# A list scheduler for the order of every engine, and byte addresses for the experts, in a two-layer encoder on eight cores

## The reference

```python
def reference(x, ...):
    h = x
    for layer in range(2):
        y = rmsnorm(h, norm_mix_g[layer])
        y = pool_attn_mixer(y, ...) if layer == 0 else sgu_mixer(y, ...)
        h = h + y
        h = h + hier_moe(rmsnorm(h, norm_ffn_g[layer]), ...)
    return rmsnorm(h, final_norm_g)

def pool_attn_mixer(h, w_in, w_pool, pool_scale, rel_bias, w_out):
    z = h @ w_in                      # 1024 x 2048: pooled channels, q, k, v
    ...                               # window means 2/4/8/16; 8 heads, own 64-frame chunk and 8 before it
    return concatenate([a_out, b_out], -1) @ w_out

def sgu_mixer(h, w_in, b_in, ln_g, ln_b, w_s, b_s, w_out):
    u, v = split(gelu(h @ w_in + b_in), 2, axis=-1)
    v = layernorm(v, ln_g, ln_b)      # then a lower-triangular 128 x 128 mix over positions, per head
    ...
    return (u * mixed) @ w_out

def hier_moe(h, ...):                 # router: best of 4 groups, best 2 of its 4 experts
    act = silu(h @ w_gate) * (h @ w_up) * combine     # 16 experts of width 256, two per token are not zero
    return act @ w_down
```

## Time and profile before

| | us |
|---|---|
| median of 3 runs | 3680.98 (3679.82 to 3682.50) |
| the profiled execution | 3689.05 |
| its span on the slowest core | 3687.1 |
| spans of the eight cores | 3668.3 to 3687.1 |

### The profile page before, as it was taken

One profiled execution on the slowest core, in us unless ns is written; L12 is line 12 of the kernel. 1 busy time (PEld: TensorE's weight loads), 2 busy tenths in 40 slices (PEclk: granted clock), 3 DMA queues, 4 the chain that ended last, 5 costly groups with the idle time before them and its releaser, 6 DMA issues. The chain is left out here.

```text
span 3687.1 us, 37878 instructions; the slowest of 8 cores (3668.3 to 3687.1 us)
## 1 busy us (share of the span) xinstructions
PE 2436.4 (66%) x10190; PEld 1001.2 (27%) x10374; DVE 1357.0 (37%) x2933; ACT 1158.2 (31%) x1864; POOL 565.7 (15%) x860
## 2 busy tenths in 40 slices
PE   0665755647574663888888466575666648888886
PEld 0222322223232231222222133343333322222221
DVE  1343433334343442222222153344443433333333
ACT  1353444444443531222222132322332212333332
POOL 1000000010000012222222111110111122333332
PEclk9876876778676776999999777777777769999998
DMA  9001101010110054355431311111111272453200
GB/s 197 23 30 39 46 23 49 20 65 27 46 37 21 29 100 91 80 116 121 106 88 45 87 35 63 63 52 69 43 50 57 59 151 77 112 129 108 68 23 1
DMA packets 88263, 243.91 MB, mean 66 GB/s; under 512 B 22360, under 2 KB 31064, under 8 KB 87568
## 3 DMA queue, kind: packets, MB, share of 16 engines
q0 software_dynamic: 57840, 130.65, 16.6%
q1 hardware_dynamic: 30240, 110.83, 9.0%
HBM read 516.19 MB, written 94.50 MB: 166 GB/s over the span
## 5 line engine op out<-in xcount | busy, mean ns | idle before, releaser
L303 PE MATMUL psum<-arena 128*128 128x512 bf16 x2979 | 836.3, 440 | 37.9 <-DVE arena L907 10.9
L610 PE MATMUL psum<-arena 128*128 x1722 | 668.9, 391 | 188.5 <-issue 106.9
L303 PEld LDWEIGHTS psum<-arena 128*128 128x128 bf16 x3072 | 327.4, 111 | 498.4 <-issue 227.1
L293 POOL TENSOR_SCALAR arena<-arena 128x1 f32<-128x1 f32 x215 | 88.3, 411 | 2075.2 <-ACT arena L391 1123.1
L373 PE MATMUL psum<-arena 128*128 128x128 bf16 x512 | 65.5, 308 | 457.0 <-DVE arena L366 381.7
L632 PE MATMUL psum<-arena 128*128 x844 | 318.5, 390 | 46.9 <-issue 4.5
L610 PEld LDWEIGHTS psum<-arena 128*128 128x128 bf16 x1760 | 168.4, 96 | 662.2 <-issue 662.2
L614 DVE SCALAR_TENSOR_TENSOR arena<-arena,psum 128x256 bf16<-128x256 f32 x220 | 105.7, 480 | 562.7 <-ACT arena L612 334.6
L612 ACT ACTIVATE arena<-psum 128x256 f32<-128x256 f32 x220 | 84.5, 384 | 625.8 <-PE psum L610 520.8
L898 PE MATMUL psum<-arena 128*128 128x512 bf16 (+3 forms) x469 | 132.7, 349 | 174.7 <-DVE arena L884 141.8
L635 DVE TENSOR_TENSOR arena<-psum,arena 128x1024 f32<-128x1024 f32 x110 | 134.7, 1225 | 291.9 <-PE psum L632 291.9
(11 more groups left out here) (170 smaller groups left out, 2785.7 us busy)
## 6 DMA issues: line engine op xcount, KB each, us to landing
arena<-wmoe POOLq DMA_DIRECT2D x114, 1536.0 KB, 46.4
arena<-x SPq DMA_DIRECT2D x64, 512.0 KB, 3.4
H<-arena SPq DMA_DIRECT2D x64, 512.0 KB, 2.8
arena<-H SPq DMA_DIRECT2D x64, 512.0 KB, 3.3
arena<-ab_w_in POOLq DMA_DIRECT2D x4, 1024.0 KB, 55.0
arena<-sgu_w_in POOLq DMA_DIRECT2D x4, 1024.0 KB, 11.7
TBL<-arena SPq DMA_DIRECT2D x2, 1536.0 KB, 23.4
arena<-gvec SPq DMA_DIRECT2D x5, 512.0 KB, 11.0
```

The costliest lines, as they stand in the source:

```text
L293: P.add("pool", lambda e: e.tensor_scalar(out=rs, in0=ss, scalar1=scale, scalar2=EPS, op0=ALU.mult, op1=ALU.add), reads=kss, writes=krs)
L303: P.add("pe", lambda e, kc=kc: e.matmul(bank(b), lhsT=lhs(kc), rhs=rhs(kc), start=(kc == 0), stop=(kc == n - 1)), reads=reads(kc), writes= ...
L610: return e.matmul(bank(b), lhsT=tT[i % 2][:, kc, :], rhs=W[:, bass.ds(v + kc * 512, 512)], start=(kc == 0), stop=(kc == 7))
```

## The change

`Prog` keeps one list of all operations. Before anything is emitted, `schedule` runs a list scheduler over the whole program: each operation has an estimated duration and latency (`estimate`, or a pair given with `add`), DMAs share one rate, and at each step the operation that can start earliest is taken, among at most 48 of an engine whose predecessors are placed; an earlier place in the program wins where starts are equal. PSUM banks are chosen there as well: a `VT` stands for a bank, or a pair, out of an allowed set, and gets it when its first operation is placed. `waits` then works out which semaphore waits are needed, leaving out those that an earlier wait implies. The hand-made interleaving is gone: the program lists stage 1, attention and output projection of a super-block in plain order, the same in layer 1, and the steps of an item one after the other in `moe`.

The expert slots are addressed in bytes, and the constant part of an address goes into the slice. The two Exp of `route` become powers of e on POOL. The last item also names all six slots as read.

```diff
+def estimate(eng, fn):
+    r = Rec(); fn(r)
+    n, a, k = r.call
...
+    if n.endswith("dma_start"):
...
+        return (1000 if eng == "pool" else 70), byts
...
+    if eng == "pe":
+        if n == "transpose":
+            f32 = a[1].dtype == F32
+            return (215 if f32 else 57), 170
+        f32 = k["lhsT"].dtype == F32
+        return (max(200, sz * 4 / 2.4) if f32 else max(57, sz / 2.4 + 3)), 170
+    if eng == "act":
+        return ((172 if ps else 224) + sz) / 1.2, 60
+    if eng == "dve":
+        return ((120 if ps else 62) + sz) / 0.96, 60
+    return 400 + sz * 1.1, 60
...
+        def pick(e):
+            best = None
+            T = free_t[e]
+            n = 0
+            for idx, op in avail[e]:
+                n += 1
+                if n > 48:
+                    break
+                st = max(T, ready[op])
+                new = [v for v in (op.vt or ()) if v.banks is None]
+                if new:
+                    if any(d.fin is None for v in new for d in v.ext):
+                        continue
+                    pl = place(new[0])
+                    if pl is None:
+                        continue
+                    st = max(st, pl[0])
+                if best is None or st < best[0] - 1.0:
+                    best = (st, op)
+                    if st <= T:
+                        break
+            return best
...
+            if op.is_dma:
+                free_t[e] = st + op.dur
+                dma_t[0] = max(dma_t[0], st + op.dur) + op.lat / 250.0
+                op.fin = dma_t[0] + 2000.0
...
-                P.add("act", lambda e: e.activation(out=T(2), in_=T(2), func=AF.Exp), reads=[kT(2)], writes=[kT(2)])
+                P.add("pool", lambda e: e.tensor_tensor(out=T(2), in0=ecst, in1=T(2), op=ALU.pow), reads=[kT(2), "ecst"], writes=[kT(2)])
...
-            W = view(slot0, [128, NSLOT * EW], BF16)
-            BT, BG, BA, BO = 0, (1, 2), (3, 4), 6
+            W = view(slot0, [128, NSLOT * EW], BF16); W8 = W.bitcast(U8)
+            BT = BG = BA = Banks(0, 1, 2, 3); BO = Banks((4, 5), (6, 7))
...
+            def wslice(e, i, x_, c):
+                return W8[:, c:c + 1024 + (NSLOT - 1) * 2 * EW][:, bass.ds(vals[(i, x_)], 1024)].bitcast(BF16)
+            def reg(e, ap, hi, mod, name):
+                r = e.alloc_register("%s_%s" % (t, name)); e.reg_load(r, ap)
+                return e.snap(r, donate=True, min_val=0, max_val=hi, guaranteed_mod_val=0, out_of_modulus=mod)
...
-                        return e.matmul(bank(b), lhsT=tT[i % 2][:, kc, :], rhs=W[:, bass.ds(v + kc * 512, 512)], start=(kc == 0), stop=(kc == 7))
+                        return e.matmul(bank(b), lhsT=tT[i % 2][:, kc, :], rhs=wslice(e, i, x_, kc * 1024), start=(kc == 0), stop=(kc == 7))
...
-                loads[i] = P.add("pool", fn, reads=["regs"], writes=[("lds", i % 8)], grp=P.group("ld%d" % (i % 8)), extra=[after] if after else [])
+                loads[i] = P.add("pool", fn, reads=["regs"], writes=[("lds", i % 8)], grp=P.group("ld%d" % (i % 8)), extra=[after] if after else [], t=(2000, 30000))
...
+            prev = None
             for i in range(NITEM):
...
                 if i + 3 < NITEM and i > 0:
-                    load_step(i, after)
+                    load_step(i, prev)
+                N(i); Tr(i)
+                E(i, 0); E(i, 1)
+                AT(i, 0); AT(i, 1)
+                prev = Dn(i)
+                if final:
+                    fin1(i); fin2(i)
+                S(i)
...
-        run_all(stage1n(0))
         for s in range(NS):
-            units = chain(*([out0(s - 1)] if s > 0 else []), *([stage1n(s + 1)] if s + 1 < NS else []))
-            n_units = (28 if s + 1 < NS else 0) + (26 if s > 0 else 0)
-            interleave(attention(s), 40 if s else 24, units, n_units)
+            run_all(stage1n(s))
+            attention(s)
+            if s + 1 < NS:
+                run_all(out0(s))
...
         for s in range(NS):
-            run_all(vstage(s))
-            if s > 0:
-                run_all(out1(s - 1))
-            run_all(ustage(s))
+            run_all(norms1(s), vstage(s), ustage(s))
...
-            if s + 1 < NS:
-                run_all(norms1(s + 1))
-            run_all(spatial(s))
+            run_all(spatial(s))
+            if s + 1 < NS:
+                run_all(out1(s))
```

386 lines of the change are left out of this document (238 added, 148 removed).

## The result

The changed kernel takes 2555.0 us in the median, against 3680.9 before: a ratio of 0.694, with an interval of 0.6928 to 0.6952. The forecast was 2507.

A forecast was written before the change was run, and what follows sets the result against it. Bounds: order in the mixers, DMA in the passages, a half-idle array in the expert stages. Start 88, mixers 880 and 596, passages 67 and 58, experts 379 and 406, between 24, end 12 give 2510, forecast 2507 us, range 2190 to 2920.

The forecast's parts named there:

- Part 1, the register sum: Expert stages: products 0.217 us apart once register work per product shrinks; stages 644 to 379 and 647 to 406 us.
- The cover of the expert reloads: Expert stages: a reload's 10 us of DMA engine time is hidden behind three items, 20 us.
- rival C: Expert stages: expert loads come late, 46 us from issue to landing against 20 of cover; total 3027 us, chance 6%.
- Part 2, layer 0's mixer: Layer 0's mixer: new order closes the 51 us hole per super-block; 105 us each, stage 1252 to 880 us.
- Part 2, layer 1's mixer: Layer 1's mixer: new order closes the hole and the 13 us wait; 72 us per super-block, stage 855 to 596.
- Part 3, banks: Banks chosen by the scheduler: gain in expert stages counted within the 6.7 us per item, in attention priced at nothing.
- Part 4, moved transfers: Passages: expert loads issued earlier leave the queue where table scatters wait; 92 to 67 us and 73 to 58.
- Part 5, the powers: Route in both mixers: powers on POOL instead of Exp on ACT, priced at 0, kept to +20 us.
- A: Array-bound products: a third clock level of thirteen sixteenths, a product taking 0.267 us; total 2765 us, chance 9%.
- B: Both mixers gain nothing; score products stand ahead of next projections among the scheduler's 48 candidates; total 3138 us, chance 10%.
- D: Expert stages: the register sum is not what the name says, products stay at 0.43 us; total 3029, chance 5%.
- E: Mixers and expert stages: the new order spreads PE's work, the clock stays at the lower level; total 3911 us, chance 4%.

The follow-up runs named there:

- Part 1 alone: The kernel before with only expert slots addressed in bytes and the constant part in the slice, hand-written order and fixed banks kept: 3244 us.
- deep buffers: The changed kernel with ten row buffers instead of six in the expert stages and scatters not waiting for the scatter before: 2480 us.
- the window: The changed kernel with the scheduler looking at 256 candidates of an engine instead of 48: 2553 us.

## Why the prediction was right in sum, and wrong in its parts

*Part 1, the register sum: right.* Products 0.216 us apart, one short operation, no assertion. Part 1 alone brings 428 us, and without reloads the stages are 367 and 402 where 379 and 406 were forecast. The bound of "about 125 ns" for what the sequencer has left was on the safe side: 32 ns of record.

*The cover of the expert reloads: wrong.* The prediction took 10 us of DMA engine time against three items of 20 us and called it covered. Two terms were missing. A gather that goes into the same queue behind a reload lands 11 us after it is issued and stands in the way of DVE's queue; the chain of scatters puts POOL's queue behind it too. And the reload may start only when the item before is done, so that in the hand order, at 5.8 us an item, hardly more than two items lie between; that it also shares the DMA engines with gathers and scatters was not taken apart. Together 79 and 76 us: rival C in its place, at 7.8 us per reload and not the 26 (46 less 20) that it was priced at, but not by its sign. In the changed kernel PE waits for a gate that stands behind a gather, and for `wmoe` only in the kernels with deep buffers or the hand order. The Trainium skill (DMA: Bandwidth & Descriptors, Two DMAs through the same engine are not ordered) says that descriptors within one queue of an engine start in order; the gather of 1086.82, late behind the reload, agrees with that, and the prediction should have weighed it.

*Part 2, layer 0's mixer: right in size, in part by luck.* Mixer and passage together are 938 us against 947, with part 5's cost in it. The super-blocks are 114 us apart, not 105, but the 40 us that were added for the stage's ends were not needed: the first has its last router product 108 us after the stage begins, and the other seven follow in 7 x 114. With the power's price mended, or the exponential on ACT, the last router product comes 30 or 20 us earlier still. The large hole is gone: of the 16.5 us waits none is left, PE's waits for the scaled block come to 12.2 us in nine in the whole stage, and the largest is now attention's own, for the bias product:

```profile
PE psum L1098 <- DVE arena L1081: 46.6, 39, 4.7
...
PE psum L582 <- DVE arena L575: 12.2, 9, 3.5
```

One of the prediction's own signs was missed: the granted clock of this mixer is 0.83, not above 0.85. The last super-block pulls it down. From 900 to 948 us PE has only attention's products, since no later super-block is left to fill in, and the last 102 us of the stage stand at 0.62:

```profile
900.00:1002.00 102.00, 69.16 (x266) 30.66 (x269) 38.08 (x137) 54.71 (x76) 13.12 (x17) 0.62 0.75 129
```

The floor of 84 us per super-block was added up at the upper level. Eight of them are 672 us, some 10 less as the first has 24 items, and PE was busy for 737, so 65 to 75 us of that are the price of the lower level, an estimate.

*Part 2, layer 1's mixer: the size was off.* A floor of 59 us per super-block was right, but 22% were put on it for packing. In the trace the last router products of successive super-blocks are 62 to 64 us apart, 5 to 8% above it (76 for the last one). A stretch of 100 us there:

```profile
1600.00:1700.00 100.00, 92.42 (x593) 55.80 (x603) 62.45 (x145) 43.44 (x65) 24.20 (x43) 0.98 0.32 112
```

PE is at 92% with DVE at 62 and ACT at 43. In layer 0 three engines stand at 81, 53 and 61% of the stage and the super-blocks are 108 to 117 us apart, 114 in the mean, 36% above their floor of 84. The prediction took 25% for the one and 22% for the other. That the loss goes with how full the next engines are fits both stages, but was not tried by itself, and the granted clock differs as well, 0.83 against 0.96.

*Part 3, banks:* priced at nothing in attention, which no run took apart. In the expert stages shared banks and fewer waits together bring 13 us in layer 0 and 2 in layer 1, under the same order of items, no more than such stages vary.

*Part 4, moved transfers: right in kind, and nearly in size.* The 24 and 41 us of the stage table begin at later work than the 92 and 73 of before. From the last router product to the first expert product 64 and 44 us became 35 and 36, 29 and 8 less, where 25 and 15 were forecast. The mechanism is the one forecast in layer 0: the table's scatters no longer queue behind the loads, and the loads have landed before the passage begins. Holding the loads back until the router is done takes away more than this gain, 53 and 45 us.

*Part 5, the powers: wrong.* "Only the last route is on the path" looked at who waits for the result, not at what stands behind that waiter on DVE, in every super-block. It cost 20 to 30 us in layer 0's mixer, at and over the +20 that was kept for it. The bound itself, 9 us for 16 elements, held (2.9).

*The rivals.* A has no support in the executions profiled here: 15 products in a row at 0.216 with all eight cores at work, expert stages at 0.97 to 0.99 granted clock where no reload holds them up. The Trainium skill (TensorE: Matmul & The Clock Gate, Part 1) states a third level of 13/16 once three cores of a die are in dense matmuls; by it these rows would, as an estimate, be at 0.267 us, and they are not. B fell, since both mixers gained, and its weak form with the window; C came in small, D and E didn't come.

So the total came out by luck: 106 us too many, nearly all from the end of layer 0's experts to the start of layer 1's, stood against 148 too few in the expert stages.

## What to carry to other kernels

A list scheduler is worth what its prices are worth: one operation priced at 418 ns that takes 2907 made a mixer some 30 us longer, and where a fixed pattern repeats 55 times a hand-written order with whole blocks of work between dependent steps was better than it. Before calling a large transfer hidden, list what goes into its queue behind it and what engine has that at its head. Check the parts of a forecast by stage even when the sum is right, and end the stages at the same work before and after.

## What was not expected of the hardware

A power on POOL costs 0.55 us in the median for one element per partition, 1.02 for four and 2.91 for sixteen, about 0.16 us for each further element. A register operation of PE's sequencer is 32 ns where the address is one sum with a known bound. ACT's table loads, by contrast, cost nothing that can be seen where PE is the limit: with the exponentials back on ACT there are 30 of them, of 1.28 us each, in layer 1's mixer in place of one, and it takes 555 us (from the last add before it to its last router product) against 553.
